# Steps spread over the gather batches by TensorE's work; key tiles placed singly; the gate's chunk ahead of the attention of blocks 2 and 3

## The reference

```python
# first layer, token_mix
proj = a @ w_in                       # split in aq, ak, av, rq, rf, ri, rg (512 columns each)
att  = diff_attention(aq, ak, av)     # 4 heads, two softmaxes a head, causal over all earlier tokens
rec  = hgrn2(rq, rf, ri) * silu(rg)   # a gated recurrence; rg is its output gate
h    = h + concat(att, rec) @ w_out
# first layer, peer_ffn, for each block of 128 tokens
q    = xb @ w_query                   # 8 heads x 2 x 128
s    = q . subkeys                    # top 16 of 128, twice, then top 16 of the 256 sums
hid  = gelu(u_table[experts] . xb) * gates      # 8 heads x 16 experts for each token
y    = sum_k hid[k] * v_table[experts[k]]
# second layer
q, k, v, z_a, u_b, v_b, z_b, g_a, g_b = split(rmsnorm(x) @ w_in_2)
y_a  = stick_breaking_attention(q, k, v) * silu(z_a)
y_b  = spatial_gating(gelu(u_b), gelu(v_b)) * silu(z_b)
x    = x + (sigmoid(g_a) * (y_a @ w_up_a) + sigmoid(g_b) * (y_b @ w_up_b)) @ w_out_2
```

## Time and profile before

| | us |
|---|---|
| median of 3 executions | 2204.71 (2201.36 to 2216.07) |
| the profiled execution, its own time | 2216.99 |
| its span, first to last instruction | 2215.2 |
| mean granted clock of TensorE | 0.884 of full |

### The profile page before, as it was taken

The page is one execution under the profiler, slowest core; times in us unless marked ns, Lnnn a source line. Parts: engine busy times, 40 slices in busy tenths (PEclk is TensorE's granted clock), DMA queues, the critical chain, the costliest instruction groups (busy, mean ns, idle before and its releaser), DMA issues.

```text
span 2215.2 us, 20759 instructions
## 1 busy us (share of the span) xinstructions
PE 1777.0 (80%) x7102; PEld 907.3 (41%) x7102; DVE 1323.3 (60%) x3450; ACT 629.6 (28%) x1225; POOL 571.2 (26%) x516
## 2 busy tenths in 40 slices
PE   7977678768898776877657989899978886776978
PEld 7545444325464342423214434443425242224443
DVE  0332778776778656676776567856565678543221
ACT  2221332313443233211124124521222254212331
POOL 0000323432322222333432222332232234230000
PEclk9977899888999877897878999799989988998869
DMA  4425999999998765899998998899999999997516
GB/s 136 137 82 175 368 407 411 380 418 367 409 399 326 286 241 217 349 419 398 421 419 350 405 380 325 350 375 418 397 388 413 417 414 366 418 417 274 209 58 217
DMA packets 132905, 739.59 MB, mean 334 GB/s; under 512 B 15792, under 2 KB 17200, under 8 KB 67264
## 3 DMA queue, kind: packets, MB, share of 16 engines
q0 software_dynamic: 73728, 536.90, 60.0%
q1 hardware_dynamic: 59072, 201.36, 24.6%
HBM read 736.11 MB, written 2.10 MB: 333 GB/s over the span
## 4 chain that ended last, share of the span: by engine, by line
PE 49%; DMA 26%; DVE 14%; ACT 6%; issue 3%; POOL 1%; SPq 0%; DVEq 0%; POOLq 0%
PE pa L662 29%; DMA uv_rows<-in_peer_uv,small 16%; DMA wbuf<-in_wt 10%; PE py L662 10%; PE pb L662 8%; DVE uv_rows L1566 4%; ACT area L1010 3%; ACT L1006 2%; POOL uv_rows L1739 1%; DVE small L1475 1%; DVE tk L1576 1%; DVE small L1553 1%; PE pb L698 1%; ACT an L1010 1%; ACT small L1010 0%
## 5 line engine op out<-in xcount | busy, mean ns | idle before, releaser
L1739 POOL DMA_INDIRECT uv_rows<-in_peer_uv,small x512 | 571.0, 1115 | 1435.3 <-PE py L662 1128.1
L1566 DVE CUSTOM_DVE_ANT_0 uv_rows<-uv_rows,xrep 128x1024 f32<-128x1024 f32 x512 | 617.8, 1223 | 303.5 <-DMA uv_rows<-in_peer_uv,small 302.6
L662 PE MATMUL py<-uv_rows,tk 128*64 128x512 f32 x2048 | 572.1, 686 | 137.1 <-DVE tk L1576 136.4
L662 PE MATMUL pa<-wbuf,area 128*128 128x512 f32 (+1 forms) x800 | 379.2, 618 | 47.6 <-DMA wbuf<-in_wt 30.7
L1010 ACT ACTIVATE small<-small 128x2 f32<-128x2 f32 (+3 forms) x324 | 69.2, 214 | 998.8 <-DVE small L1566 989.2
L662 PEld LDWEIGHTS py<-uv_rows,tk 128*64 128x64 f32 x2048 | 137.9, 151 | 459.0 <-issue 251.0
L662 PEld LDWEIGHTS pa<-wbuf,area 128*128 128x128 f32 (+1 forms) x800 | 144.9, 191 | 270.7 <-issue 209.8
L662 PE MATMUL pa<-area,wbuf 128*128 128x128 f32 (+2 forms) x1280 | 215.4, 330 | 8.9 <-DMA wbuf<-in_wt 4.1
L662 PEld LDWEIGHTS pa<-area,wbuf 128*128 128x128 f32 x1280 | 194.1, 214 | 40.5 <-issue 20.1
L662 PE MATMUL pb<-wbuf,area 128*128 128x512 f32 x384 | 183.8, 624 | 26.5 <-DMA wbuf<-in_wt 15.0
L1010 ACT ACT_TABLE_LOAD x133 | 170.6, 1283 | 28.2 <-PE pa L662 20.3
(11 more groups left out here) (179 smaller groups left out, 1177.7 us busy)
## 6 DMA issues: line engine op xcount, KB each, us to landing
wbuf<-in_wt SPq DMA_DIRECT2D x352, 512.0 KB
uv_rows<-in_peer_uv,small POOLq DMA_INDIRECT x512
wbuf<-in_skT SPq DMA_DIRECT2D x16, 256.0 KB
h<-in_x SPq DMA_DIRECT2D x4, 512.0 KB, 11.0
fw<-in_finw SPq DMA_DIRECT2D x4, 512.0 KB
out<-h SPq DMA_DIRECT2D x4, 512.0 KB, 6.2
an<-in_x SPq DMA_DIRECT2D x3, 512.0 KB, 5.7
uv_rows<-in_finw SPq DMA_DIRECT2D x2, 512.0 KB, 6.3
```

Of the source, the lines that this page charges most:

```text
L662: return nc.tensor.matmul(o, l, r, start=start, stop=stop, skip_group_check=True)
L1566: last = V.tensor_tensor_reduce(uv_rows[:, n % RING, 0:D], uv_rows[:, n % RING, 0:D], xrep[:, b % 2, n % TG, :], 1.0, 0.0, ALU.mult, ALU.a ...
L1739: nc.gpsimd.indirect_dma_start(uv_rows[:, n % RING, :], None, t["peer_uv"], bass.IndirectOffsetOnAxis(ap=expert_ids[:, c:c + 1].bitcast(U3 ...
```

## The change

It touches only the order of the plan; every step, tile, buffer and wait rule stays.

1. `mixing_rows`: for the group (2, 3) the four `rg` tiles stand behind `rotq` and ahead of the attention, one to a row (the first beside `rotq`). Groups of one block keep them in the first two rows of the attention.
2. `tensor_work(s)` gives each step a number for TensorE's work, and `spread` lays rows by the sum of it (at least 2 a row) and puts a row at most one batch behind the row ahead of it. Rows of little work can share a batch.
3. `place_keys` lays each of the 5 key steps of a pair singly: within 16 batches ahead of the first need, each in the batch with the least work, at its first spot with nothing open.
4. The ranges of `spread` move: groups (2, 3) end at batch 109 and not 105; the second layer's (0, 1) ends at 206 and not 202.

```diff
@@ mixing_rows
-        rows += weave(chain, proj) + [[("rotq", g)]]
+        rows += weave(chain, proj) + [[("rotq", g)] + rg[0:1]] + pairs_of(rg[1:], n)
...
-    att[0] = att[0] + rg[0:1]
-    att[1] = att[1] + rg[1:4]
+    if len(g) == 1:
+        att[0] = att[0] + rg[0:1]
+        att[1] = att[1] + rg[1:4]
@@
+def tensor_work(s):
+
+    if len(s) == 1:
+        return 0
+    name, g = s[0], s[1]
+    nb = len(g) if isinstance(g, tuple) else 1
+    if name in COLS_IN or name in COLS_2:
+        return KT * nb / 4
+    if name in ("wq", "sc"):
+        return KT / 4
+    if name in ROWS_IN or name in ROWS_2 or name in ("ga", "gb", "out", "wo", "ua", "ud"):
+        return 2 * nb
+    nk = 0 if isinstance(g, tuple) else g + 1
+    return {"norm1": 2, "n3": 2, "xt": 4, "rotk": nb, "rotq": nb, "lm": 2, "kdt": 1, "st": 3, "r3": 1, "a3": 1, "us": nk,
+            "ut": nk / 4, "uv": nk / 4, "zs": nk / 2, "zt": 1, "zv": 1, "sg": 2, "yt": 2, "mt": 2}.get(name, 0)
+
+
+LEAST = 2
+
+
 def spread(rows, lo, hi, ticks):
 
-    for r, row in enumerate(rows):
-        ticks[lo + r * (hi - lo) // len(rows)] += row
+    work = [max(LEAST, sum(map(tensor_work, row))) for row in rows]
+    done, at = 0, lo - 1
+    for row, w in zip(rows, work):
+        at = min(at + 1, lo + int((done + w / 2) * (hi - lo) / sum(work)))
+        ticks[at] += row
+        done += w
@@
+def place_keys(ticks):
+
+    chunk, gaps = Open(), []
+    for row in ticks:
+        free = [] if chunk.now() else [0]
+        for i, s in enumerate(row):
+            chunk.add(s)
+            free += [] if chunk.now() else [i + 1]
+        gaps.append(free[:1])
+    work = [sum(map(tensor_work, row)) for row in ticks]
...
+    for b in range(NB):
+        for i in range(4):
+            need = PER_HEAD * (HP * b + 2 * i - LEAD) - 1
...
+            lo = max(last, inputs_at.get(b, 0) + 1, need - 2 * PER_HEAD + 1)
+            for j, s in enumerate(steps):
+                end = lo + max(1, (need - lo) // (len(steps) - j))
+                spots = [k for k in range(lo, end) if gaps[k]] or [k for k in range(lo, len(ticks)) if gaps[k]][:1]
+                k = min(spots, key=lambda k: work[k])
...
@@ make_plan
-    spread(mixing_rows((2, 3)) + input_rows(2) + [[("xt", 2)]], q3, PER_BLOCK + q3, ticks)
+    spread(mixing_rows((2, 3)) + input_rows(2) + [[("xt", 2)]], q3, PER_BLOCK + q3 + 4, ticks)
-    spread(second_rows((0, 1)), 2 * PER_BLOCK + 6, 3 * PER_BLOCK + 10, ticks)
-    spread(second_rows((2,)), 3 * PER_BLOCK + 10, n, ticks)
+    spread(second_rows((0, 1)), 2 * PER_BLOCK + 6, 3 * PER_BLOCK + 14, ticks)
+    spread(second_rows((2,)), 3 * PER_BLOCK + 14, n, ticks)
+    place_keys(ticks)
...
-        pending += keys.get(k, [])
-        room = 2 if len(pending) > 2 else 4
-        for s in [None] + ticks[k]:
...
+        out += ticks[k]
```

More of the change, by code:

```diff
@@ L125, in mixing_rows @@
     rows += second + [[("fq", g)]]
+    rg = tiles("rg", g)
     proj = tiles("ri", g) + tiles("ak", g) + tiles("av", g) + tiles("aq", g)
@@ L134, in mixing_rows @@
         chain[15].append(("rotk", g))
-        rows += weave(chain, proj) + [[("rotq", g)]]
+        rows += weave(chain, proj) + [[("rotq", g)] + rg[0:1]] + pairs_of(rg[1:], n)
     units = [(b, hh) for b in g for hh in range(HA)]
     att = [sorted(row, key=lambda s: s[0] == "ut") for row in pipeline(units, [["us"], ["ue"], ["uw"], ["ut"], ["uv"]], 2)]
-    rg = tiles("rg", g)
-    att[0] = att[0] + rg[0:1]
-    att[1] = att[1] + rg[1:4]
+    if len(g) == 1:
+        att[0] = att[0] + rg[0:1]
+        att[1] = att[1] + rg[1:4]
     for k, b in enumerate(g):
@@ L246, in add @@
             self.scores = s[0] == "us"
+def place_keys(ticks):
[7 more added lines that the diff above has]
+    work = [sum(map(tensor_work, row)) for row in ticks]
+    inputs_at = {s[1]: k for k, row in enumerate(ticks) for s in row if s[0] == "xt"}
+    inputs_at[0] = 0
+    chosen, last = [[] for _ in ticks], 0
+    for b in range(NB):
+        for i in range(4):
+            need = PER_HEAD * (HP * b + 2 * i - LEAD) - 1
+            if need < 0:
+                continue
+            steps = ([("xt", b)] if (b, i) == (3, 0) else []) + key_steps(b, i)
+            lo = max(last, inputs_at.get(b, 0) + 1, need - 2 * PER_HEAD + 1)
[3 more added lines that the diff above has]
+                k = min(spots, key=lambda k: work[k])
+                chosen[k].append(s)
+                work[k] += tensor_work(s)
+                lo = k
+            last = lo
+    for k, steps in enumerate(chosen):
+        if steps:
+            ticks[k][gaps[k][0]:gaps[k][0]] = steps
 def make_plan():
@@ L256, in make_plan @@
     spread(mixing_rows((1,)) + input_rows(1) + [[("xt", 1)]], 0, q3, ticks)
-    spread(mixing_rows((2, 3)) + input_rows(2) + [[("xt", 2)]], q3, PER_BLOCK + q3, ticks)
+    spread(mixing_rows((2, 3)) + input_rows(2) + [[("xt", 2)]], q3, PER_BLOCK + q3 + 4, ticks)
     spread([[("ldpost",)], *input_rows(3), [("ldfin1",)]], 2 * PER_BLOCK, 2 * PER_BLOCK + 5, ticks)
-    spread(second_rows((0, 1)), 2 * PER_BLOCK + 6, 3 * PER_BLOCK + 10, ticks)
-    spread(second_rows((2,)), 3 * PER_BLOCK + 10, n, ticks)
[L261 to L267, removed]
+    spread(second_rows((0, 1)), 2 * PER_BLOCK + 6, 3 * PER_BLOCK + 14, ticks)
+    spread(second_rows((2,)), 3 * PER_BLOCK + 14, n, ticks)
+    place_keys(ticks)
+    out = []
     for k in range(n):
@@ L287, in make_plan @@
         out += [("mix", k)] + ([("rows", k - 1)] if k % PER_BLOCK else [])
-    assert not pending
     return first + out + [("ldlast",), ("rows", n - 1)] + [("take", NB - 1)] + flat(second_rows((3,)))
```

## The result

The changed kernel takes 2201.0 us, the kernel before 2212.5 us in the same series (20 runs each): ratio 0.9948, 95% interval [0.9926, 0.9971]. So it is about 11.5 us faster where the forecast said 26, and 0.5% is within what I had called no change. The profiled run took 2208.1 us.

The account below looks back on a forecast made before the run. The prediction took DMA engines' idle time as the bound, 118.7 us at most to gain. Its terms summed to 24 us, plus 2 for batches 59 to 61: 26 off the 2204.7 median gives 2179 us, range 2146 to 2208.

Parts of the forecast that it names:

- (c): 1174 to 1339 us: lumps of TensorE work shrink, though n2 and n3 share a batch twice; +3 us, between -6 and +8.
- (d): 1339 to 1430 us, second block's attention, groups 0 and 1: doubled pipeline rows lose 19 us against 13.5; -6, between -14 and +3.
- (g): Key tiles changing places, including wq ahead of norm1 in batches 41 and 42: costed at nothing, covered by gathers in flight.
- (e): 1430 to 1843 us, nearly full already: +2 us of the 4.1 lost there.
- the term for batches 59 to 61: Overfull batches 59 to 61, in 220 to 660 us, come apart: +2 us.
- What bounds it: Whole kernel: bytes unchanged, so time changes only by DMA idle time; at most 118.7 us, two thirds in 742 to 910.
- (a): 742 to 910 us, attention of blocks 2 and 3: rg before the scores and keys spread; +25 us, between +10 and +55.
- (b): 660 to 742 us, recurrence of block 3: tiles load in idle DMA time; +3 us, between -4 and +6.
- (f): 1843 to 1855 us and batches around, same pipeline for block 2 of the second part: -3 us, between -12 and +1.
- D: Whole kernel: stall goes, but key steps show in the attention and doubled rows cost more; 2202 us, chance 0.23.
- B: Attention of blocks 2 and 3: goes at DMA's pace once empty ring and low clock are cured; 2149 us, chance 0.16.
- C: Evenly filled batches: TensorE falls to the lower clock; 2229 us, chance 0.13.

Follow-up runs that it names:

- e6: The changed kernel, but rows with zs, zd, ze, zt or zv never share a batch with another such row; ratio 0.9877 to the kernel before.
- e4: The changed kernel with the old spread by number of rows again, all else kept; ratio 0.9892 to the kernel before.
- e1: The kernel before with only the rg tiles of blocks 2 and 3 moved ahead of their attention; ratio 0.9972 to the kernel before.
- e2: The changed kernel with rg of blocks 2 and 3 put back in the attention's first rows; ratio 1.0007 to the kernel before.
- e7: The changed kernel, with key tiles behind the norm's steps, not ahead, in batches 41 and 42; ratio 0.9965 to the kernel before.
- e9: e8 with the rg tiles put back among the first attention rows; ratio 0.9820 to the kernel before.
- e5: The changed kernel, but rows with n1, m1, n2 or n3 never share a batch with another row; ratio 0.9909 to the kernel before.
- e8: The changed kernel with every chain row alone in its batch, keys behind the norm, weight-tile rows sharing batches; 2164.7 us, ratio 0.9805 to the kernel before.
- e3: The changed kernel with key tiles laid by the old rule, block 2's first group two batches later; ratio 0.9978 to the kernel before.

## Why the forecast was too high

The step that failed is the price of rows that share a batch. The prediction saw the form in (c) and (d), used its one measured example, for (d) alone, gave (c) a gain all the same, priced the norms of block 2 in no term, and put the key tiles ahead of `norm1` at nothing in (g). Together (c), (e), (g) and the term for batches 59 to 61 were to give 7 us; by the ledger they took 18.

- **What bounds it** held. The bytes are the same, and lost DMA time goes with the time: 123.8, 118.6, 99.9, 84.9 us lost go with ratios 1, 0.9948, 0.9892, 0.9805. It does not order kernels that lie close together: e6 loses more than e4 (101.8) and is faster (0.9877), and e1, e2 and e7 lose more than before (126.2, 129.5, 124.5) without being slower. One wrong turn of that ledger: my sum covered 220 to 1855 us in seven pieces and took the stages that lost nothing as safe. Two of them (to the second layer, and the norms of block 2) lose 6.8 and 7.4 us after. And the attention held 64.9 of 118.7 us, a little over half, not two thirds.
- **(a), +25: the size was right by the ledger, the split was not seen.** 64.9 us became 34.7, so +30. No idle of TensorE stands before `rg0`, and the four `rg` batches took 24.1 us at full clock where I forecast 27. The attention's batches 79 to 96 took 147.9 us against 138.7, for 22 batches in 172 us, not 166. Counted as (a) was built, in batches of gathers, that is 24.9 - 4.5 = 20 us; the ledger counts the weight tiles that load there too. Four windows of the changed kernel: the `rg` batches, two batches of block 2, two rounds of block 3:

```profile
750.30:774.40 24.10, 24.10 (x71) 8.74 (x70) 19.77 (x48) 4.14 (x9) 9.71 (x9) 1.00 1.02 419
...
813.70:833.00 19.30, 12.13 (x48) 5.76 (x48) 14.42 (x38) 5.99 (x16) 4.92 (x5) 0.82 0.70 259
...
852.00:872.70 20.70, 14.01 (x59) 8.84 (x60) 12.52 (x38) 7.65 (x24) 4.75 (x4) 0.75 0.87 319
872.70:894.90 22.20, 15.37 (x63) 7.61 (x61) 12.42 (x33) 9.45 (x25) 3.89 (x4) 0.81 0.62 218
```

  Paired as in the prediction, the rounds took 14.8, 21.7 and 11.8 us (block 2), 15.7, 20.7, 22.2 and 12.3, not 15.5 three times, 13 and 17.4 three times; the time did not come out as I built it, only the lost share did. I had taken one measured round of each kind for all of its kind. And by e2 and e9 half or less of it is `rg`. The rest I put down to rows that came apart, above all those of batches 77 and 86, which held two rows of the attention's chain before, took 18.7 and 17.5 us and lost 11.2 and 12.7; no run took these two apart alone.
- **(b), +3:** 8.9 to 6.3, +2.6. Right.
- **(c), +3: wrong in sign.** I saw that `n2` and `n3` share a batch "twice" and gave them no price of their own, only less give-back from the lumps. In fact the norms of groups 0 and 1 went from 2.7 to 8.9 us and their projections from 8.1 to 6.7: -5, inside (c)'s bounds but not its sign. The norms of block 2, which lie in the stretch of (e), share batches too and went from 0 to 7.4; no term had them. e5 shows the cause: with those rows alone both losses vanish. The row to price it by was in front of me, and I used it only for (d).
- **(d), -6:** -8.6. The mechanism and nearly the size; three batches of 10.4, 11.4 and 10.9 us, as the earlier trace rows had said.
- **(e), +2:** +6.3 in batches 172 to 205, -7.4 in the norms of block 2: -1. **(f), -3:** +1.4 more lost in that pipeline, -1.4.
- **(g), "costed at nothing": -5 and -6.8.** Batches 41 and 42 got the keys ahead of the norm and lost 7.7 us, where they had lost about 4; "covered by gathers in flight" held for neither. e7 shows 4.5 us of batch 41 to be the keys' place. Another 3.6 us are lost in batch 53, behind batch 52, which holds `lx` and `ly` of block 2 and takes 16.0 us. In e8, with each of these rows alone and the keys behind the norm, the stage loses nothing at all; the two were not tried apart there. The +2 for the batches 59 to 61 drowned in it. Of the 6.8 us ahead of the second layer, 4.2 are batch 109, where the rule puts four `wq` at once. They are not what loses it: e3 has two there and loses 4.3, and in the changed kernel TensorE reaches them only behind the `py` matmuls that GpSimd waits for:

```profile
991.39 7.09 PE L706 MATMUL pa<-ident,xrep 128*128 128x64 f32 x32 [3.93 <-ACT xrep L1054]
998.40 3.04 PE L706 MATMUL py<-uv_rows,tk 128*64 128x512 f32 x8
1001.37 0.82 PE L706 MATMUL pa<-xnT,wbuf 128*128 128x128 f32 x5
```

  Ahead of `py` stand the transposes of `xt` of block 2 and the wait for ScalarE before them, and GpSimd waited 11.73 us in all. Before, the same step is followed by two batches that lose 2 us. Why it costs 2 to 3 us more after was not tried; `x2` and `x3` share a batch ahead of it.
- **Sum:** 30 (a) + 3 (b) - 5 (c) - 9 (d) - 1 (e) - 1 (f) - 12 (g) = 5 us of ledger, 11.5 us by the runs. Forecast was 26. (g) with the batches 59 to 61 misses by 14 us, (c) by 8, (d) and (e) by 3 each; (a) was 5 better.
- **The rivals.** What came was nearest to D, "the doubled rows cost more than I take", 2202 us. But D had its loss at the wrong place: the key steps in the attention showed nothing worth naming. B is out (share 0.76 in the attention; one round took less than 12 us, but the mean of the seven was 17). C is out as well: the granted clock was 0.95 in 668 to 774, 0.97 in 1176 to 1344 and 0.98 in 1434 to 1658, where each batch holds 4 units or little more, so it stood nearly always at the upper of its levels (2.4 GHz). It fell where TensorE waited for ScalarE (0.63 in 1144 to 1176). The Trainium skill ("TensorE: Matmul & The Clock Gate", section "HAM oscillation — how this bites in real kernels") warns against small portions of matmuls between waits for DMA. Those stretches do not test it: TensorE was busy for 97.62 of 106, 156.78 of 168 and 204.81 of 224 us there, so it hardly waited. I had read it as a warning against small portions, and it is one against the waits between them; the 0.50 and 0.69 of batches 135 and 136, with 5.27 us of waiting for ScalarE in the second, agree with it in kind.

## What to carry to other kernels

Where the engines run one list of steps in order beside a stream of transfers, a step's price is not the busy time of the dearest engine but the length of the chain of waits it hangs in. Here rows of a chain over several engines wanted a slot each, even where they cost TensorE nothing, and rows of plain weight tiles could be stacked. Before costing a move at nothing, look in the plan after for every slot that holds two dependent rows, and price each by the one example that the trace of before has.
